# The last two expert rows taken one by one, and the second block's residual and norm moved ahead of a weight split

## The reference

```python
# peer_ffn, per block of 128 tokens
u = expert_down[eidx]                        # 128 experts per token: 8 heads x 16
a = jax.nn.gelu(jnp.einsum('thkd,td->thk', u, xb), approximate=False)
coef = (g * a.astype(jnp.float32)).astype(xb.dtype)
return jnp.einsum('thk,thkd->td', coef, expert_up[eidx])
# end of the first block
h = h + peer_ffn(rmsnorm(h, g_ffn[l]), ...)
return rmsnorm(h, g_final)
# start of the second block
h = rms_norm(x, norm_mix[i])
u = h @ w_in[i]
(gq, gk, gv, g_lr, g_r, mq, mk, mv, gate_a, gate_b) = jnp.split(u, points, axis=-1)
```

## Time and profile before

| | us |
|---|---|
| median of 3 executions | 1396.29 |
| lowest, highest | 1394.45, 1397.71 |
| the profiled execution | 1396.57 |
| its span, first to last instruction | 1394.8 |
| mean granted clock of TensorE | 0.984 of full |

### The profile page before, as it was taken

How to read it: one execution, slowest core, us unless ns; L and a number is a source line. 1 busy time by engine, 2 the same in 40 slices (tenths; PEclk the granted TensorE clock), 3 DMA queues, 4 the chain that set the end, 5 groups by cost and what they waited for, 6 DMA issues and landing times.

```text
span 1394.8 us, 15362 instructions
## 1 busy us (share of the span) xinstructions
PE 1263.4 (91%) x5520; PEld 867.3 (62%) x5520; DVE 947.4 (68%) x1974; ACT 587.1 (42%) x1047; POOL 277.6 (20%) x281
## 2 busy tenths in 40 slices
PE   8999999798888888788787778799999999999998
PEld 8888898443343433334343234388688888888887
DVE  5657657876777777777777776655666656877445
ACT  4657453333123232322322233465556744554334
POOL 1000001443435334344434334100000000000000
PEclk9999999899999999989999999999999999999999
DMA  7443536999999999999999999845354445455551
GB/s 287 164 176 108 183 129 260 419 381 421 420 421 410 423 421 421 421 406 421 418 422 421 421 416 421 316 158 186 121 181 153 163 167 181 171 193 181 190 203 61
DMA packets 57267, 398.73 MB, mean 286 GB/s; under 512 B 7128, under 2 KB 7640, under 8 KB 9448
## 3 DMA queue, kind: packets, MB, share of 16 engines
q0 software_dynamic: 36864, 268.45, 46.5%
q1 hardware_dynamic: 18288, 126.10, 25.3%
q10 hardware_dynamic: 2040, 3.19, 0.7%
HBM read 396.67 MB, written 1.05 MB: 285 GB/s over the span
## 4 chain that ended last, share of the span: by engine, by line
PE 58%; DMA 25%; DVE 8%; ACT 6%; issue 2%; POOL 1%; ACTq 0%; SPq 0%; DVEq 0%; POOLq 0%
PE ps L853 36%; DMA B<-in_ex,eidx 24%; PE ps L1225 10%; PE ps L881 4%; DVE B L2566 3%; PE ps L882 2%; ACT hl L1502 2%; DVE hl L2082 1%; DMA ring<-in_wt 1%; ACT diags L1778 1%; POOL B L817 1%; ACT L1767 1%; ACT av_ L1771 1%; PE ps L1103 0%; ACT L1771 0%
## 5 line engine op out<-in xcount | busy, mean ns | idle before, releaser
L1225 PE MATMUL ps<-B,diags 128*128 128x512 f32 x1024 | 486.7, 622 | 110.0 <-ACT diags L1778 108.0
L1225 PEld LDWEIGHTS ps<-B,diags 128*128 128x128 f32 x1024 | 191.3, 196 | 376.6 <-issue 201.8
L817 POOL DMA_INDIRECT B<-in_ex,eidx x256 | 271.5, 1061 | 600.3 <-PE ps L1225 359.0
L2566 DVE CUSTOM_DVE_ANT_0 B<-B 128x1024 f32<-128x1024 f32 x256 | 311.3, 1221 | 112.0 <-DMA B<-in_ex,eidx 111.4
L2082 DVE TENSOR_TENSOR hl<-ring,hl 128x2048 fp32r<-128x2048 f32 x110 | 251.7, 2290 | 174.1 <-ACT hl L1502 173.9
L1502 ACT ACTIVATE hl<-ring 128x2048 fp32r<-128x2048 f32 x110 | 210.3, 1913 | 129.5 <-PE ps L853 126.7
L853 PE MATMUL ps<-hl,R 128*128 128x512 f32 x912 | 212.0, 391 | 0.3 <-DVE R L2098 0.3
L853 PE MATMUL ps<-hl,XT 128*128 128x512 f32 (+1 forms) x888 | 203.9, 388 | 2.7 <-DVE hl L2082 2.2
L1771 ACT ACTIVATE av_<-av_ 128x2 f32<-128x2 f32 x128 | 26.0, 203 | 422.1 <-DVE av_ L2566 422.0
L853 PEld LDWEIGHTS ps<-hl,R 128*128 128x128 f32 x912 | 169.9, 188 | 36.0 <-DVE R L2098 0.7
L853 PEld LDWEIGHTS ps<-hl,XT 128*128 128x128 f32 x888 | 162.5, 188 | 38.3 <-issue 3.1
(11 more groups left out here) (374 smaller groups left out, 1017.6 us busy)
## 6 DMA issues: line engine op xcount, KB each, us to landing
ring<-in_wt SPq DMA_DIRECT2D x112, 1024.0 KB, 4.8
raw<-in_wt SPq DMA_DIRECT2D x4, 1024.0 KB, 6.6
B<-in_ex,eidx POOLq DMA_INDIRECT x256
X<-in_x SPq DMA_DIRECT2D x2, 512.0 KB, 4.4
B<-in_mem ACTq DMA_DIRECT2D x1, 1024.0 KB, 8.5
PW<-in_wple SPq DMA_DIRECT2D x1, 1024.0 KB, 7.5
ring<-in_wt SPq DMA_DIRECT2D x2, 512.0 KB, 4.2
out<-B SPq DMA_DIRECT2D x3, 256.0 KB, 2.4
```

What stands on the lines that cost most here:

```text
L817: e.indirect_dma_start(out=rows[i % NG][:, :], out_offset=None, in_=A["ex"], in_offset=bass.IndirectOffsetOnAxis(ap=eidx[:, tb, s:s + 1], ...
L1225: m = e.matmul(acc[tb][hf][:, :], diags[:, i % 4, :], rows[i % NG][:, 1024 + 512 * hf:1536 + 512 * hf], start=(s == 0), stop=(s == 127))
L2566: m = e.tensor_tensor_reduce(R[:, 0:1024], R[:, 0:1024], XG[:, tb, :], 1.0, 0.0, ALU.mult, ALU.add, av_[:, tb, s + z:s + z + 1])
```

## The change

Two things are changed.

First, for i = 254 the pair isn't treated as a pair. VectorE takes row 254's dot product, counts up `one_dot`, waits for the GELU of that one column (`one_gelu`), multiplies it (`one_coef`), and then does the same for row 255. ScalarE (`last_rows`) does the GELU and the diagonal of each row by itself.

Second, behind the rows, VectorE does the residual and the gain product of block 1 between the two quarters of gv(0,0), and no longer splits gv(0,1) before the norm; both gv(0,1) and gv(1,0) are split after the norm's root. ScalarE splits gv(0,1) after the root, not ahead of the squares; the root comes ahead of the split of gv(1,0) as well, and the two small loads come between the two splits.

```diff
@@ scalar engine
+            def last_rows():
+                for z in range(2):
+                    c = av_[:, 1, 126 + z:127 + z]
+                    e.wait_ge(*one_dot[z])
+                    e.activation(c, c, ACT.Gelu).then_inc(one_gelu.sem)
+                    e.wait_ge(*one_coef[z])
+                    e.wait_ge(*pe["ex", 250 + z])
+                    e.activation(diags[:, (254 + z) % 4, :], ident[:, :], ACT.Copy, scale=c).then_inc(dgx.sem)
...
-                        if i > 0:
+                        if i == 254:
+                            last_rows()
+                        elif i > 0:
                             row_gelu(i, tb, s)
                             row_diagonals(i, tb, s)
...
             n = NUM["gv", 0, 0]
             split_first()
-            split_to(n + 1)
             e.activation(small[:, 61:62], epsc[:, :], ACT.Sqrt)
             final_sum(1)
             final_gained(1)
-            e.wait_ge(*sqs["final", 1])
+            sqrt(("final", 1))
+            split_to(n + 1)
             fetch("ggn", GB[:, :], A["ggn"].partition_broadcast(128))
             fetch("gw2", gw2, A["gw2"])
             split_to(n + 2)
-            sqrt(("final", 1))
             for k in range(2):
                 final_turned(1, k)
@@ vector engine
+                        if i == 254:
+                            for z in range(2):
+                                R, c = rows[(i + z) % NG], slice(s + z, s + z + 1)
+                                e.wait_ge(*gath[i + z])
+                                e.tensor_tensor_reduce(R[:, 0:1024], R[:, 0:1024], XG[:, tb, :], 1.0, 0.0, ALU.mult,
+                                                       ALU.add, av_[:, tb, c]).then_inc(one_dot.sem)
+                                e.wait_ge(*one_gelu[z])
+                                e.tensor_tensor(av_[:, tb, c], av_[:, tb, c], gw[:, tb, c], ALU.mult).then_inc(one_coef.sem)
+                            first_block(n)
+                            continue
...
             for c, ready_hi, m in ((slice(0, 1024), gv_hi[0], gv_lo), (slice(1024, 2048), hi[n], lo)):
                 e.wait_ge(*ready_hi)
                 e.tensor_tensor(w[1][:, c], loaded(n)[:, c], w[0][:, c].bitcast(F32), ALU.subtract).then_inc(m.sem)
-            residual_sum(1)
-            gain_sum(1)
-            split_to(n + 1)
+                if c.start == 0:
+                    residual_sum(1)
+                    gain_sum(1)
             final_var(1)
             final_root(1)
             split_to(n + 2)
```

More of the change, by code:

```diff
@@ L337, in program @@
         dgx = count("dgx", range(256))
+        one_dot = count("one_dot", [0, 1])
+        one_gelu = count("one_gelu", [0, 1])
+        one_coef = count("one_coef", [0, 1])
         glrs = count("glrs", [0])
```

## The result

| | before | after |
|---|---|---|
| median of 16 executions each | 1394.99 | 1398.14 |
| lowest, highest | 1390.92, 1397.96 | 1396.09, 1400.36 |
| the profiled execution | 1396.57 | 1399.44 |
| its span | 1394.8 | 1397.7 |
| mean granted clock | 0.984 | 0.980 |

The ratio is 1.0021 [1.0013, 1.0029]: 2.9 us slower, with an interval from 1.8 to 4.0. The time is the forecast one (1398.0) within 0.2 us, but that is luck: before's own median came out 1.3 lower over sixteen executions than over three. The difference is larger than the +1.7 that was forecast, and above the +1.0 to +2.4 that I had given to the forecast's own case. The interval leaves zero out, and the ratio lies on the bound of what I had called measurable.

What follows compares the result with a forecast made beforehand. After row 255 a stream of weight matmuls on PE sets the pace. Durations +0.4 us (row and norm gains used up) plus 1.3 for the clock make +1.7: 1398.0 against the median, range 1394.8 to 1400.5.

Steps and rivals of the forecast that it cites:

- the forecast's own case: One low clock stretch around the edit, costing +1.0 to +2.4 us in all; chance 0.47.
- the clock's 1.3 us: PE's two new waits bring one stretch at half clock, of about 3.4 us, losing 1.3 us of matmul work.
- The yardstick: When PE starts the first matmul of gv(1,0), 908.70 in before; a shift goes nearly whole into the span.
- w2: Weight half gv(1,0), which PE multiplies after the transposes of block 1; start forecast at 909.1 for 908.70.
- Part 1, the rows: Last two rows: taken one by one, row 255 ends at 895.6 instead of 897.1, a gain of 1.5 us.
- w1: Weight half gv(0,1), which PE multiplies before the transposes of block 1; start forecast at 904.6 for 901.99.
- this sign of being right: In the rows: row 255 ends near 895.6 on before's time scale.
- Part 2, the order: Behind the rows: w1 queued behind the norm uses up both gains, so PE starts w2 +0.4 us later.
- the norm's 4.5 us: Block 1's norm: its diagonal is ready at 901.9 instead of 906.45, 4.5 us earlier for the transposes.
- rival two: Around PE's new waits: clock still low after the second, or low for a double stretch; +3.2 to +3.7 us; chance 0.15.
- Rival three: The edit pays: PE reaches w2 earlier than in before; 1395.9, or 1394.8 at the large end; chance 0.10.
- Slower by over 0.2%: Whole kernel measurably slower, by more than 2.8 us: most of rival two and some smaller cases; chance 0.16.

Runs made afterwards that it cites:

- e6: after, with PE's transposes of block 1 moved ahead of w1's matmuls; ratio to before 1.0002.
- e1: after with only the rows one by one, the order behind them on both engines as in before; ratio to before 0.9996.
- e4: after, with w1's split ahead of the squares on ScalarE and ahead of the variance on VectorE; ratio to before 0.9995.
- e5: after once more, unchanged, on another chip; ratio to before 1.0021.
- e8: Rows one by one, VectorE's tail as in before; ScalarE loads the Sqrt table ahead of w1's split and takes the root ahead of w2's; ratio to before 0.9999.
- e11: e10 with five dummy matmuls on PE ahead of row 252 and six ahead of gv(0,0)'s second quarter; ratio to before 0.9984.
- e3: after, with dummy matmuls filling PE's two new waits: 7 ahead of gv(0,0)'s second quarter, 12 ahead of w1; ratio to before 1.0012.
- e7: after, with VectorE doing both quarters of gv(0,0)'s low part ahead of the residual, as in before; ratio to before 1.0031.
- e9: after with dummy matmuls on PE in three waits: 5 ahead of row 252, 7 ahead of gv(0,0)'s second quarter, 12 ahead of w1; ratio to before 1.0007.
- e2: before, with after's new order behind the rows on both engines, rows 254 and 255 still a pair; ratio to before 1.0020.
- e10: Rows one by one, with the scalar order of e8 and the vector order of e4; ratio to before 0.9992.

## Why the prediction was right, and where it was not

**Forecast +1.7 us, measured +2.9 (1.8 to 4.0).** The time fell in the range and on the forecast side. The structure held; one term, the clock's 1.3 us, was too small. The close agreement of the time itself is luck, as said above.

**The yardstick held.** I judged the edit by when PE starts w2 and said that a shift goes nearly whole into the span. It does: 280.5 to 280.6 us from w2 to the up projection in every profile in which w2 follows the transposes. after's span adds up as 888.43 + 24.82 + 280.6 + 88.9 + 115.0 = 1397.75, before's as 888.91 + 19.79 + 280.6 + 90.5 + 115.0 = 1394.8. The profiled pair differs by 5.0 us in the way to w2, of which 1.6 is hidden by the up projection's other pace and 0.5 by T0; neither belongs to the change, and the ratio over all executions says 2.9. e6 warns of the same: 2.1 us later than before at w2 in its profile, and no slower by its ratio of 1.0002.

**Part 1, the rows: gain 1.5 us, true, and of no use.** T0+6.7 for T0+8.2 in e1, e4, e5 and e8 to e11. The forecast said that it is used up in the new order. e1 shows that it was worth nothing in the old one either, since w1's transfer and ScalarE's chain don't start from PE. What the forecast left out is that it isn't safe: in after, e3, e6 and e7 the clock was low at the rows, and row 255 then ends at T0+8.4, so in after's own profile this sign of being right is missing. A wait of 1.93 to 1.98 us stands ahead of row 252 in all eleven profiles that don't fill it, before's among them; the clock fell behind it in those four. The change doesn't make this wait. Whether it makes the fall more frequent isn't settled by so few.

**Part 2, the order: +0.4 us, right.** Diagonal at T0+13.0 (e5; 13.0 forecast; 14.7 in after's profile, where the rows end late), w1 at T0+15.7 (e5, e9; 15.7 forecast), waits of 2.17 and 3.51 us (2.2 to 2.5 and 3.7), the transposes without a wait behind w1, w2 at T0+20.26 at full clock (e9; 20.2 forecast). The cause I named is shown: w1, which PE needs first, is queued behind the norm. Moving only w1 forward (e4) takes the loss away, and so does moving PE's transposes ahead of it (e6). That the norm's 4.5 us are real is shown by e5 (the diagonal at T0+13.0 for 17.5), and that PE's order is what leaves them unused is shown by e6.

**The clock: +1.3 us, too small.** This is the term that was mis-sized. A single low stretch did cost about what I took: w2 at 21.84 in e5 is 1.6 above the 20.2 of the durations. But in after's profile and e2's the clock fell 1.1 and 0.6 us behind the end of the first wait and was low through the second and all of w1, for 10.2 us; e6 has 6.8 us of it, and so has e7 with its one long wait. That is rival two's mechanism, with 0.15. At w2 it costs 24.82 - 21.94 = 2.9 us (after against e3, both with the low clock in the rows). Of two profiles of after, one shows the forecast's case and one the rival's. The rows' low stretch comes on top and takes the row's gain away (row 255 at 8.4, w1 at 17.4 for 15.7). The two may hang together: where the rows end late, the first new wait is 2.45 to 2.47 us and the clock fell behind it (after, e2, e6), and where they end at T0+6.7 it is 2.17 to 2.19 and the clock held (e4, e5, e10). Six profiles don't prove that.

Taking each case half the time, the tail gives 0.4 + (1.6 + 2.9)/2 = 2.65, and half of the 1.7 of the rows makes 3.5; measured is 2.9, and some 1.9 of it is the clock by e9. The half is a guess. Two profiles of after are too few, one of them above its median by 1.3 us and one below by 2.5. Nor is it known how often before's own clock is low around the edit, since it has one profile; a loss of its own there would make the measured difference smaller than this sum.

**What in the reading led to the small term.** In before's trace eleven of twelve waits of 2.2 us and more were followed by a fall and none of the three just below, and so I took 2.2 us for where it begins. Over all thirteen profiles, the kernel's very first wait left out, it isn't so: 15 of 35 waits of 1.9 to 2.2 us were followed by a fall, 48 of 78 of 2.2 to 2.6, 67 of 88 of 2.6 and more. Three rows of one execution were too few to put a chance on a short wait, and the wait of 1.94 us in the rows belonged in the sum.

**Two slips in the sums.** Rival three's 1395.9 should read 1396.0, and of the low stretch up to 1.7 us (0.8 + 0.9) and not 1.5 could lie in the wait, so that the loss begins at 0.7 and not at 0.8. Neither moves the forecast.

**Chances.** Slower by over 0.2% had 0.16, most of it for the long low stretch. With a ratio of 1.0021 the outcome is at that bound; with the price that the runs show for the clock, I would now give "slower" about a half.

## What to carry to other kernels

Where engines work in order, look at which of two results the consumer takes first. To bring the second forward at the cost of the first gains nothing, however large the gain is by itself (here 4.5 us), unless the consumer's order is turned with it. Before moving a step to fill one wait, count the price of the wait that it opens twice: its length, and the half clock of what PE does behind it; matmuls without use in such waits gave back some 1.9 of 2.9 us here, by a rough estimate. And measure from an anchor next to the edit: two profiles of the same kernel differed by 3 us at w2 and by 2 at T0.

## What was not expected of the hardware

**The up projection has two paces at full clock.** Its matmuls of 512 columns, 256 on one line (count, shortest/median/longest ns, from and to; the counts behind the forms are of a sample), in before:

```profile
L881 PE MATMUL ps<-XT,hl x256: 387/398/502, 1189.3 to 1279.8; 128*128 128x512 f32 x128
```

and in after:

```profile
L884 PE MATMUL ps<-XT,hl x256: 391/391/498, 1193.8 to 1282.7; 128*128 128x512 f32 x128
```

Each is followed by one of 256 columns on the next line. A pair takes 0.353 us in the one and 0.347 in the other, and the stage 90.5 or 88.8 to 88.9 us. The difference is all in the larger one: from start to start it has a median of 236 or 230 ns, and the smaller one 117 ns in both. It goes by execution and not by kernel: seven of the thirteen profiles have the one (before, e4, e5, e6, e7, e10, e11), six the other, and after has had both. The granted clock is 1.00 in each. I don't know the cause; it makes 1.65 us of the scatter that every comparison here has to beat.

**The same wait doesn't always bring the same clock.** The wait ahead of row 252 is 1.98 us in after and in e8, with the same work before it. In after the clock is at 0.50 from 0.2 us behind its end for 3.4 us, and the four rows take 1.7 us longer; in e8 it stays at 1.00:

```profile
887.97 8.83 PE L1228 MATMUL ps<-B,diags 128*128 128x512 f32 x16 [1.98 <-ACT diags L1781]
```

```profile
887.29 7.13 PE L1228 MATMUL ps<-B,diags 128*128 128x512 f32 x16 [1.98 <-ACT diags L1781]
```
